# Attention stage: two modulation chunks after each batch and four beside the output product, and the output product in whole fp32

## The reference, cut to what matters

```python
mod = jax.nn.silu(c) @ w + b                  # 1024 -> 3072: shift, scale, gate
...
h = x * (1.0 + scale) + shift
qkv = h @ w_in
...
probs = (p / denom).astype(v.dtype)
o = jnp.einsum("bnhgqj,bnjhd->bnqhgd", probs, vb)
y = o.reshape(B, S, N_Q_HEADS * HEAD_DIM) @ w_out      # 256x1024 by 1024x1024
...
x = layer_norm(DN_ALPHA * x + (1.0 + gate) * y, ln_g[i, 0], ln_b[i, 0])
shift, scale, gate = ada_modulation(c, ada_w[i, 1], ada_b[i, 1])
y = sq_relu_mlp(x * (1.0 + scale) + shift, mlp_w1[i], mlp_w2[i])
```

## Time and profile before

| | |
|---|---|
| median of 3 runs | 1676.21 us |
| lowest, highest | 1666.42, 1679.6 us |
| the profiled execution's own time | 1678.0 us |
| its span, first to last instruction | 1676.7 us |
| TensorE matmul busy | 1376.2 us (82%) |
| VectorE busy | 1159.0 us (69%) |
| ScalarE busy | 719.8 us (43%) |
| mean granted TensorE clock | 0.913 |
| chain that ended last | PE 61%, DVE 29%, ACT 6%, issue 2%, DMA 2% |

### The profile page before, as it was taken

How to read it: one execution, slowest core, us unless ns; L and a number is a source line. 1 busy time by engine, 2 the same in 40 slices (tenths; PEclk the granted TensorE clock), 3 DMA queues, 4 the chain that set the end, 5 groups by cost and what they waited for, 6 DMA issues and landing times.

```text
span 1676.7 us, 20860 instructions
## 1 busy us (share of the span) xinstructions
PE 1376.2 (82%) x7808; PEld 1200.5 (72%) x7808; DVE 1159.0 (69%) x1541; ACT 719.8 (43%) x896; POOL 63.1 (4%) x54
## 2 busy tenths in 40 slices
PE   0862799997999977888985998655789999888885
PEld 0752799996777756888974797544777777777674
DVE  6657677776577567788766656985465557777775
ACT  2332335442565663334432333111244445666663
POOL 1100010000000001000000000430000000000000
PEclk9985999999999988999987998886889999999998
DMA  8425487874566445665760463100054556878782
GB/s 350 151 75 213 151 258 277 286 260 145 201 235 219 163 145 210 227 218 184 273 217 20 144 208 126 39 0 10 1 204 146 179 178 220 298 263 299 269 300 77
DMA packets 84069, 311.90 MB, mean 186 GB/s; under 512 B 9344, under 2 KB 9568, under 8 KB 83360
## 3 DMA queue, kind: packets, MB, share of 16 engines
q1 hardware_dynamic: 82080, 298.88, 51.1%
q10 hardware_dynamic: 1888, 11.69, 2.1%
HBM read 309.48 MB, written 1.05 MB: 185 GB/s over the span
## 4 chain that ended last, share of the span: by engine, by line
PE 61%; DVE 29%; ACT 6%; issue 2%; DMA 2%; DVEq 0%; POOL 0%; ACTq 0%; SPq 0%; POOLq 0%
PE ps L388 60%; DVE w_low L347 10%; DVE junk L347 5%; ACT w_high L347 2%; DVE t_one L347 1%; DVE t_two L347 1%; DVE rs L347 1%; DVE he L347 1%; DVE qp L347 1%; DMA ring<-stream 1%; DVE x L347 1%; PE ps L856 1%; DMA ring<-moe 1%; DVE sc L347 1%; DVE pf L347 1%
## 5 line engine op out<-in xcount | busy, mean ns | idle before, releaser
L347 DVE TENSOR_TENSOR w_low<-ring,w_high 128x1024 fp32r<-128x1024 f32 x376 | 461.6, 1228 | 196.2 <-ACT w_high L347 170.4
L347 ACT ACTIVATE w_high<-ring 128x1024 fp32r<-128x1024 f32 x376 | 398.9, 1061 | 327.1 <-PE ps L388 276.3
L388 PE MATMUL ps<-x_high,w_high 128*128 128x256 f32 (+1 forms) x784 | 235.8, 301 | 79.2 <-DVE x_low L347 71.6
L388 PE MATMUL ps<-x_low,w_high 128*128 128x256 f32 (+1 forms) x784 | 233.0, 297 | 0.0
L388 PE MATMUL ps<-x_high,w_low 128*128 128x256 f32 (+1 forms) x784 | 232.7, 297 | 0.0
L388 PEld LDWEIGHTS ps<-x_high,w_high 128*128 128x128 f32 x784 | 154.5, 197 | 90.5 <-issue 84.2
L347 DVE CUSTOM_DVE_ANT_0 junk<-ring,cond 128x1024 f32<-128x1024 f32 x133 | 165.3, 1243 | 20.9 <-DMA ring<-stream 3.6
L388 PE MATMUL ps<-h_high,w_high 128*128 128x256 f32 x512 | 147.7, 289 | 10.9 <-DVE h_low L347 10.9
L388 PEld LDWEIGHTS ps<-x_high,w_low 128*128 128x128 f32 x784 | 154.5, 197 | 2.8
L388 PEld LDWEIGHTS ps<-x_low,w_high 128*128 128x128 f32 x784 | 154.7, 197 | 2.5
L388 PE MATMUL ps<-h_low,w_high 128*128 128x256 f32 x512 | 146.9, 287 | 0.0
(11 more groups left out here) (299 smaller groups left out, 2170.3 us busy)
## 6 DMA issues: line engine op xcount, KB each, us to landing
ring<-stream SPq DMA_DIRECT2D x376, 512.0 KB, 4.6
ring<-moe SPq DMA_DIRECT2D x192, 512.0 KB, 4.6
tab_two<-tab ACTq DMA_DIRECT2D x1, 2824.0 KB, 14.1
gw<-gw ACTq DMA_DIRECT2D x1, 2304.0 KB, 13.3
cond<-cvec ACTq DMA_DIRECT2D x3, 512.0 KB, 6.8
x<-xT ACTq DMA_DIRECT2D x1, 1024.0 KB, 12.0
ctx<-ctxT ACTq DMA_DIRECT2D x1, 1024.0 KB, 4.8
pos<-posT ACTq DMA_DIRECT2D x1, 1024.0 KB, 6.9
```

The lines of the kernel that those rows point to most:

```text
L347: return op(*a, **k).then_inc(self.sem, 1)
L388: return pe.matmul(out, stationary, moving, start=start, stop=stop, skip_group_check=True)
```

## The change

In the stream, four of the twelve chunks of `a` that came ahead of the output weights now alternate with them: two pieces of `w`, two of `a`, four times. VectorE does two modulation chunks after each batch instead of three, and one chunk ahead of each of the four pairs of additions. The bias is added in two parts (8 columns ahead of `gate1`, 16 columns behind the last addition). The eight output weights are no longer split: TensorE multiplies the fp32 pieces from the ring by `ot` itself, and `o_high` and `o_low` are gone. The wait ahead of the product is on ScalarE's fourth copy to `ot`. The splits of the first four MLP weights are made by VectorE behind the last addition. Pieces used whole are left out of the numbering of the split slots.

```diff
-    order = pieces("a" * 8 + "w" * 6 + "a" * 12 + "w" * 4 + mlp)
+    order = pieces("a" * 8 + "w" * 6 + "a" * 8 + "wa" * 4 + mlp)
...
-SPLIT = [w for w in range(W_END) if not W_RNN <= w < W_MLP1]
+WHOLE = [W_ATT <= w < W_MLP0 or W_RNN <= w < W_MLP1 for w in range(W_END)]
+SPLIT = [w for w in range(W_END) if not WHOLE[w]]
...
 def load_program
-            if kind == "w" and W_RNN <= n < W_MLP1:
+            if kind == "w" and WHOLE[n]:
                 sp.wait_ge(s.used, n + 1)
...
 def tensor_program
-    pe.wait_ge(s.o_low, 2)
-    project(W_ATT, m.OTS)
+    pe.wait_ge(s.ot, 4)
+    for n in range(KT):
+        piece = whole(W_ATT + n)
+        for k in range(KT):
+            ins = mm(PS[:, 4 + n // 2, (n % 2) * 256:(n % 2 + 1) * 256], piece[:, k * P:(k + 1) * P], m.OT[:, k, :], k == 0, k == KT - 1)
+        ins.then_inc(s.used, 1)
...
 def scalar_program, attend
-        A(m.OT[:, 4 * g:4 * g + 4, b * P:(b + 1) * P], PS[:, n, :].rearrange("p (h q) -> p h q", h=4), ACT.Copy)
-        if b:
-            A(m.OTS[0][:, 4 * g:4 * g + 4, :], m.OT[:, 4 * g:4 * g + 4, :], ACT.Copy, s.o_high)
+        A(m.OT[:, 4 * g:4 * g + 4, b * P:(b + 1) * P], PS[:, n, :].rearrange("p (h q) -> p h q", h=4), ACT.Copy, s.ot)
...
 def vector_program, attend
-        if b:
-            vv.wait_ge(s.o_high, g + 1)
-            k = slice(4 * g, 4 * g + 4)
-            op(vv.tensor_tensor, m.OTS[1][:, k, :], m.OT[:, k, :], m.OTS[0][:, k, :].bitcast(F32), ALU.subtract, inc=s.o_low)
...
-        for _ in range(3):
+        for _ in range(2):
             modulation(m.junk)
-    bias(16, 24, "ada_b", 16)
+    bias(16, 8, "ada_b", 16)
     op(vv.tensor_scalar, m.gate1, m.MOD[:, 16:24], 1.0, None, ALU.add)
     vv.wait_ge(s.x_next, 4)
-    project(W_ATT, m.gate1)
+    for n2 in range(4):
+        modulation(m.junk)
+        vv.wait_ge(s.used, W_ATT + 2 * n2 + 2)
+        for n in (2 * n2, 2 * n2 + 1):
+            add_branch(n, PS[:, 4 + n2, (n % 2) * 256:(n % 2 + 1) * 256], m.gate1[:, n:n + 1])
+    bias(24, 16, "ada_b", 24)
+    low_upto(W_MLP0 + 4)
```

More of the change, by code:

```diff
@@ L121, in split_upto @@
 def split_upto(w):
-    return w - max(0, min(w, W_MLP1) - W_RNN)
+    return w - sum(WHOLE[:w])
 X_MOE = 40
@@ L151 @@
     t2 x_high x_low x_add x_next
-    qk_out rope_mm rope_ps qk v_out score_mm sc smax exp prob pt_mm pt pv_mm o_high o_low
+    qk_out rope_mm rope_ps qk v_out score_mm sc smax exp prob pt_mm pt pv_mm ot
     mean_mm xc sq var_mm root
@@ L216, in __init__ @@
         self.OT = kt(view("ot", a0 + 7168, 2048))
-        self.OTS = (kt(rounded("o_high", a0 + 9216, 2048)), kt(rounded("o_low", a0 + 11264, 2048)))
         self.RT = view("rt", a0 + 13312, 512, 32)
@@ L408, in out_tile, with whole @@
         ins.then_inc(s.used, 1)
+    def whole(w):
+        c = W_AT[w]
+        pe.wait_ge(arrived[c % RING], 16 * (c // RING + 1))
+        return m.piece(c)
     def second_product(w, src_half, first, p=P):
@@ L532, in tensor_program @@
     layer_norm(1)
[L535 to L539, removed]
     def z_of(b):
```

## The result

| | before | changed |
|---|---|---|
| median | 1676.75 us (11 runs) | 1657.53 us (11 runs) |
| lowest, highest | 1666.42, 1679.6 us | 1649.55, 1658.92 us |
| ratio, 95% interval | | 0.9899 (0.9876 to 0.9922) |
| profiled execution, its span | 1678.0, 1676.7 us | 1658.18, 1656.9 us |

The changed kernel is faster by 1.0%, 17 us by the ratio and 19.2 us by the medians. Forecast was -16.6 us, and a median of 1660. The times of the kernel before lie in two groups (four from 1666.4 to 1667.0, seven from 1676.2 to 1679.6), and the ratio mixes them: the seven upper ones have the median 1678.5, the nine upper ones of the changed kernel (1656.8 to 1658.9) 1658.2, which is 20.3 us less, and the two profiled executions are 19.8 us apart.

What follows compares the result with a forecast made beforehand. Attention was taken as set by waits around VectorE, what follows by TensorE. Product start -24.5, dearer product +5.4, later mean +2.5 gave -16.6 us: 1661.4 for the profiled execution, 1660 for the median, range 1651 to 1669.

Steps and rivals of the forecast that it cites:

- (a): First attention batch: two modulation pieces fewer gain nothing, since VectorE already waited 0.49 us for TensorE's scores.
- (b): Second batch without o_low: VectorE takes the third batch's scores at 122.5 instead of 131.84, 9.4 us earlier.
- (c): Third batch: four pieces instead of six, 2.8 us more gained; TensorE's work just fits, by 0.3 us.
- (d): Behind the fourth batch: o_high, o_low, pieces, bias and first split leave the path; product starts 24.5 us earlier, at 142.2.
- (e): Output product in whole fp32: 28.2 us plus 2.4 for half clock, 30.6 in all, 5.4 longer; sign 28 to 31.
- (f): Beside the product: 15 us of VectorE pieces and additions are hidden under 30.6 us of TensorE, cost nothing.
- (g): Ring loads beside the product: weights land in time (5 to 7.7 us), no charge, but a thin margin.
- (h): Ahead of the layer norm: mean starts 6.1 instead of 3.65 us after the product, 2.5 lost (bounds 1.5 and 7.7).
- the one with the clock: Clock already up at the product's start saves 2.4 us, from the third batch another 2.9: 1655 to 1658; chance 0.22.
- the late stream: Output weights land late beside the product: 3.8 us stall twice and colder clock, about 8 us, 1668; chance 0.18.
- the half clock throughout: Output product stays at half clock, 52 instead of 30.6 us, kernel at about 1682; chance 0.03.
- the change without effect: Product still starts late because another engine, for instance ScalarE with its exponentials, replaces VectorE; chance 0.04.

Runs made afterwards that it cites:

- e4: The kernel before, unaltered, traced a second time in one execution; 1668.51 us.
- e1: Changed kernel with the modulation chunks put back (three after each batch, all twelve ahead of the output weights), product still whole fp32; 1663.64 us, ratio to before 0.9937.
- e9: e6 plus unread matmuls in the pauses of the second and third layer norm; 1640.36 us, ratio to before 0.9808.
- e6: e3 plus unread matmuls in the first layer norm's pause and ahead of the first three batches' transposes; 1646.0 us, ratio to before 0.9809.
- e7: Changed kernel with the output product held back behind eight unread VectorE multiplications (10.3 us); timed in one execution, product 29.92 us instead of 27.89.
- e8: Changed kernel with the eight modulation pieces beside the product summing only 64 of 1024 columns; 1650.02 us in one execution.
- e3: Changed kernel with the four MLP splits spread: one ahead of the mean, one in the square root's wait, two behind x_low; 1651.31 us, ratio 0.9894.
- e10: The kernel of e3 again, run beside the changed kernel on the same chip; 1652.64 us, ratio 0.9855.

## Why the prediction was right, step by step

The place was right, and so were the waits ahead of the product and their new releasers. That the measured ratio says -17 us and the forecast -16.6 is in part luck: like compared with like the gain is about 20 us (20.3 between the upper groups, 20.1 at the first MLP tile against e4, 19.8 between the spans). The start of the product came 2.3 us earlier than forecast and the product cost 2.9 less, both by the clock; the mean and the variance sums took back 0.7 and 1.5. e4 is the trace to compare with, since it runs in step with the changed kernel up to the attention; the first trace gives.

(a) *First batch: nothing.* Right. VectorE's wait grew from 0.49 to 4.24 us.

(b) *Second batch, 9.4 us.* Right: 9.1 us at the third transposes. The releaser of VectorE's third scores is TensorE, as said, at 122.73 for 122.5.

(c) *Third batch, 2.8 us more.* Right: 2.7 (11.8 in all). The fit by 0.3 us that the step worried over came out as 0.39 us of idle time ahead of the fourth transposes.

(d) *Start of the product, 24.5 us earlier.* 26.8 against e4 (25.6 against the first trace, whose first two batches ran faster). The missing 2.3 us are the fourth batch at full clock: transposes 1.20 for 1.97 us, value product 2.05 for 3.78. This was written down as a rival, with a price of 2.9 for it; it should have been the main case. The step itself had the fourth transposes follow the third batch within 0.3 us, and in all eight traces where that pause was at most 0.74 us the fourth batch ran at full clock, while with one of 2.99 us or more (before, e4, e1, e9) its transposes took 1.97. In e6, with 1.39, the transposes ran at full clock and the value product mostly not.

(e) *The product, 5.4 us longer.* The step that failed in size. At 0.217 us a row it took 27.7 us, as the 28.2 for full clock said, but the 2.4 us for a slow start did not come. Against the first trace's 25.2 us that is +2.5. e7 shows that the 2.4 was the price of a pause (2.0 measured) and that the product itself was priced right. In e1, where the fourth value product still ran at half clock, the product started at full clock all the same, 27.89 us. The 27.9 us lie a little below the 28 to 31 that were named as the sign. For whole fp32 the Trainium skill ("FP8 and Floating Point Precision", "TensorE Precision Notes") gives four passes. The trace shows two rows of 0.217 us a matmul and no passes, so it neither confirms nor refutes the number; the estimate of 30.2 us, which gave each of four passes the 0.118 us of a split matmul, came out too high.

(f) *Work beside the product: nothing.* Right, shown by e8.

(g) *The stream: nothing.* Right. TensorE has no gap in the product at 298 GB/s. VectorE waited for ring pieces there, up to 1.25 us at a time, which cost nothing.

(h) *The mean, 2.5 us later.* 3.2 (6.84 for 3.65). The size was near, the reason was not the one given. The step let the landing of the fourth MLP piece set the end, but VectorE's own queue did: the four splits stand back to back (169.15 to 174.38, 1.33 us apart), and the fourth piece's rounding had ended at 172.82, before the third split was done (173.05). In e1 all four pieces were rounded 2.2 us ahead of the product's end (169.85, 172.01), and the mean still started 6.63 us after it. The sum had counted three splits for VectorE (5.2 us); with the fourth it is 6.4, so the lower bound of 1.5 us was too low. What the step lacked is what the later mean does to TensorE: a pause of 5.09 us for one of 1.91, behind which the variance sums took 1.5 us more (1.4 more again in e8, behind the same pause). e3 and e10 take both away by moving the splits alone.

*The MLP passes everything on.* Right: first to second root 207.1 before, 207.0 after.

The sum by the traces, against the first one: -25.6 (product's start, counted from VectorE's first scores, at 92.02 and 90.75), +2.5, +3.2, +1.5 = -18.4 us, and the rest of the 19.8 us between the spans (1.3) lies ahead of the attention, where no instruction was changed. Against e4 the product's start is 1.2 us more, which is the clock in the first two batches.

Of the rivals, the one with the clock came true, at 0.22; the late stream, the half clock throughout and the change without effect did not.

## What to carry to other kernels

A subtraction of 1.2 us can cost seven times its length (9.1 us in the second batch) when it stands in an in-order queue ahead of work that others wait for: look at what is queued behind the wait, then ask whether the product may take the unsplit operand while its engine is idle anyway. When pauses of TensorE are removed, price the work behind them at the clock that continuous work has in the trace, not at the clock behind the old pause; when a pause is made longer, charge the work behind it too. When a wait ends behind several operations of one in-order engine, count all of them before blaming the load. Splits that are due soon but not yet belong into waits that exist, not between the last addition and the mean.

## What the runs showed of the hardware

Executions of the kernel before fall into two groups 10 us apart, and the traces put the difference into the later stages, with TensorE's granted clock (129.9 or 126.0 us for the same 784 matmuls, clock 0.91 or 0.93); the first MLP stage repeats within 1.1 us (206.1 to 207.2) in the kernels that leave its start as it was. Behind one and the same pause of 9.4 us the granted clock was anything from 0.50 (e4) to 0.75 (e3) over the first 6.1 us of that MLP, and the variance sums behind a pause of 1.9 us took 3.72 or 5.41. A comparison of two such kernels by a few runs is blurred by that, and so is one of whole stages; batch by batch, one trace of each told more than ten runs.

Small matmuls whose result nobody reads can raise the clock of the real work behind them: at the start of the recurrent block (15.84 to 14.07 us, a pause of 1.84 us left), and for two of four value products (3.78 to 2.05). Where they left a pause of 3.1 us they did nothing that the traces show.
